# First attention of a two-block decoder: heads in pairs on half tiles of the array, mask and maximum in one VectorE instruction, softmax divided by its sum ahead of the turn, V stationary

## What is computed

```
qkv = h @ w_qkv                       # 32 query heads, 4 key/value heads, head width 64
q, k = rms_norm per head, then rope
scores = q @ k^T * 64**-0.5           # window of 128: block t=0 sees 128 keys, block t=1 sees 256
m = max(max(scores), sink)            # one learned sink a head
p = exp(scores - m)
probs = p / (sum(p) + exp(sink - m))
out = (probs @ v) @ w_o
x = x + out
```

## Time and profile before

| | us |
|---|---|
| time, median of 3 runs | 2516.59 (2515.07 to 2518.73) |
| time of the profiled execution | 2517.14 |
| its span | 2515.6 |
| TensorE busy (matmul) | 2457.2 (98%) |
| VectorE busy | 1805.7 (72%) |
| ScalarE busy | 1174.5 (47%) |
| mean granted TensorE clock | 0.992 of full speed |

### The profile page before, as it was taken

One profiled execution on the slowest core, in us unless ns is written; L12 is line 12 of the kernel. 1 busy time (PEld: TensorE's weight loads), 2 busy tenths in 40 slices (PEclk: granted clock), 3 DMA queues, 4 the chain that ended last, 5 costly groups with the idle time before them and its releaser, 6 DMA issues.

```text
span 2515.6 us, 30924 instructions
## 1 busy us (share of the span) xinstructions
PE 2457.2 (98%) x11300; PEld 2022.6 (80%) x11300; DVE 1805.7 (72%) x2444; ACT 1174.5 (47%) x1574; POOL 41.5 (2%) x62
## 2 busy tenths in 40 slices
PE   7999999999999999999999999999999789999998
PEld 6888888888888888788888888888888678888886
DVE  6655677787777787577777777778776676666655
ACT  5555544434444444454444443444444454455553
POOL 1100000000000000000000000000000000000000
PEclk9999999999999999999999999999999899999999
DMA  6433688888888887467777687767777447776653
GB/s 222 126 103 116 202 288 282 292 285 299 284 293 285 295 286 263 144 206 236 238 231 234 226 264 246 242 228 241 230 234 238 152 146 249 250 236 214 224 188 125
DMA packets 160245, 575.00 MB, mean 229 GB/s; under 512 B 17984, under 2 KB 20288, under 8 KB 160096
## 3 DMA queue, kind: packets, MB, share of 16 engines
q1 hardware_dynamic: 159280, 570.80, 68.7%
q0 software_dynamic: 816, 2.23, 0.3%
HBM read 570.86 MB, written 2.10 MB: 228 GB/s over the span
## 4 chain that ended last, share of the span: by engine, by line
PE 91%; DVE 5%; ACT 2%; issue 1%; DMA 0%; POOL 0%; SPq 0%; DVEq 0%; ACTq 0%
PE PS L926 28%; PE PS L928 28%; PE PS L927 28%; PE PS L545 2%; DVE WL L1861 1%; ACT WH L1280 1%; ACT AR L1072 0%; PE PS L621 0%; PE PS L645 0%; ACT SQ L960 0%; DVE AR L1384 0%; DVE YA L1542 0%; PE PS L885 0%; PE PS L886 0%; PE PS L832 0%
## 5 line engine op out<-in xcount | busy, mean ns | idle before, releaser
L1861 DVE TENSOR_TENSOR WL<-W,WH 128x1024 fp32r<-128x1024 f32 x816 | 991.6, 1223 | 525.9 <-ACT WH L1280 518.0
L1280 ACT ACTIVATE WH<-W 128x1024 fp32r<-128x1024 f32 x816 | 857.3, 1059 | 862.7 <-PE PS L928 855.5
L926 PE MATMUL PS<-WH,XTH 128*128 128x512 f32 x2144 | 861.6, 402 | 6.1 <-ACT WH L1280 3.2
L928 PE MATMUL PS<-WH,XTL 128*128 128x512 f32 x2144 | 838.7, 391 | 0.0
L927 PE MATMUL PS<-WL,XTH 128*128 128x512 f32 x2144 | 837.4, 391 | 0.0
L926 PEld LDWEIGHTS PS<-WH,XTH 128*128 128x128 f32 x2144 | 404.0, 188 | 91.2 <-issue 7.9
L928 PEld LDWEIGHTS PS<-WH,XTL 128*128 128x128 f32 x2144 | 403.6, 188 | 86.7
L927 PEld LDWEIGHTS PS<-WL,XTH 128*128 128x128 f32 x2144 | 404.6, 189 | 83.0 <-issue 3.8
L926 PE MATMUL PS<-WH,YTH 128*128 128x512 f32 x1120 | 442.9, 395 | 7.2 <-DVE YTL L1397 3.2
L928 PE MATMUL PS<-WH,YTL 128*128 128x512 f32 x1120 | 437.0, 390 | 0.0
L927 PE MATMUL PS<-WL,YTH 128*128 128x512 f32 x1120 | 436.5, 390 | 0.0
(11 more groups left out here) (267 smaller groups left out, 1242.3 us busy)
## 6 DMA issues: line engine op xcount, KB each, us to landing
W<-in_ada SPq DMA_DIRECT2D x192, 512.0 KB, 4.5
W<-in_avoz SPq DMA_DIRECT2D x192, 512.0 KB, 4.4
W<-in_wg SPq DMA_DIRECT2D x88, 512.0 KB, 4.8
W<-in_wu SPq DMA_DIRECT2D x88, 512.0 KB, 4.7
W<-in_wd SPq DMA_DIRECT2D x88, 512.0 KB, 5.0
W<-in_kada SPq DMA_DIRECT2D x64, 512.0 KB, 4.6
W<-in_aqk SPq DMA_DIRECT2D x64, 512.0 KB, 4.6
W<-in_aout SPq DMA_DIRECT2D x64, 512.0 KB, 4.4
```

Source lines behind the costliest of these rows:

```text
L926: e.matmul(p, x, WH[:, g % NH, j], start=first, stop=False)
L928: i = e.matmul(p, y, WH[:, g % NH, j], start=False, stop=last)
L1280: e.activation(WH[:, n % NH], W[:, i % NW], ACT.Copy).then_inc(s_hi, 1)
L1861: e.tensor_tensor(l, src, h.bitcast(F32), ALU.subtract).then_inc(s_lo, 1)
```

## The change

It touches the first attention alone.

- 24 units become 12 pairs of banks (`PAIRS`): for each group one of 8 heads for t=0, two of 4 heads for t=1. Even heads lie in rows 0 to 63 and odd ones in rows 64 to 127; the keys are kept once in both halves (K2). A score matmul uses 64 rows, even and odd heads alternate, and write two different banks.
- The mask matmul and the two memsets of KE and KO are gone. VectorE adds the mask, scales and takes the maximum together with the sink in one `tensor_tensor_reduce` a head, which writes the scaled scores to SBUF; each gives two instructions, the second reads the accumulator. ScalarE's exp then works in place in SBUF.
- A new step `scale` three ticks after the score: VectorE adds the sink's exp to the sum, inverts it, and multiplies all 1024 columns of the pair.
- `turn` transposes 8 tiles into two banks, five ticks after the score. `pv` has V stationary (64 columns) and the turned probabilities moving (512 or 256 columns), with the result already turned, in the two column halves of the array: the division, the turn of the result and `out_T` are gone.
- `attn_q` handles both row blocks one tick apart on VectorE; scores come at least 4 ticks apart; the pauses are 2 ticks and not 4.

```diff
@@ attention_order
-    while pn < 24:
+    while pn < 12:
         if pn < tn and k >= turned[pn] + 3:
             pv(pn)
             pn += 1
-        if tn < sn and tn < pn + 3 and k >= scored[tn] + 4:
+        if tn < fn and tn < pn + 2 and k >= scored[tn] + 5:
             turn(tn)
...
-        if (sn < 24 and sn < tn + 3 and k >= last + (2 if sn % 3 else 1)
-                and (sn // 6, UNITS[sn % 6][0]) in qready):
+        if fn < sn and k >= scored[fn] + 3:
+            scale(fn)
+            fn += 1
+        if sn < 12 and sn < tn + 2 and k >= last + 4 and (sn // 3, PAIRS[sn % 3][0]) in qready:
             score(sn)
@@ TensorE
-                    msk = mrow[:, 128 - 128 * t:256].unsqueeze(1).to_broadcast([128, len(hs), k])
-                    e.matmul(b[:, :].rearrange("p (a k) -> p a k", k=k), idb[:], msk, start=True, stop=False)
-                    for x, h in enumerate(hs):
-                        K = KE if h % 2 == 0 else KO
-                        i = e.matmul(b[:, k * x:k * x + k], QT[:, t, h // 2], K[:, g, 0:k], start=False,
-                                     stop=(x == len(hs) - 1))
+                    for x in range(n):
+                        for a, (b, full) in enumerate(banks):
+                            h = slice(64 * a, 64 * a + 64)
+                            i = e.matmul(b[:, k * x:k * x + k], QT[h, t, j0 + x], K2[h, g, 0:k], start=True, stop=True)
...
-                            i = e.matmul(b[:, 64 * h:64 * h + 64], PT1[N % 3][:, q:q + 128],
-                                         V1[:, k, 64 * g:64 * g + 64], start=(k == 0), stop=(k == t))
...
+                    for k in range(1 + t):
+                        for a in range(2):
+                            i = e.matmul(b[64 * a:64 * a + 64, 128 * j0:128 * j0 + m], V1[:, k, 64 * g:64 * g + 64],
+                                         PT[P % 2][a][:, m * k:m * k + m], start=(k == 0), stop=(k == t))
@@ ScalarE
-                        i = e.activation(PBL[N % 3][:, k * x:k * x + k], b[:, k * x:k * x + k], ACT.Exp,
-                                         scale=sm(u, 3)[:, h:h + 1], bias=sm(u, 6)[:, h:h + 1],
-                                         accum_out=sm(u, 7)[:, h:h + 1])
...
+                            i = e.activation(p, p, ACT.Exp, bias=sm(u, 6)[:, h:h + 1], accum_out=sm(u, 7)[:, h:h + 1])
@@ VectorE
-                e.memset(KE[64:128], 0.0)
-                e.memset(KO[0:64], 0.0).then_inc(s_kz, 1)
...
-                    step(e.tensor_reduce(mx, b[:, :].rearrange("p (a k) -> p a k", k=k), AX.X, ALU.max))
...
+                            i = e.tensor_tensor_reduce(PB[P % 2][:, 512 * a + k * x:512 * a + k * x + k],
+                                                       b[:, k * x:k * x + k], mrow[:, 128 - 128 * t:256],
+                                                       sm(u, 3)[:, h:h + 1], rows[:, RS + 8 * g + 2 * (j0 + x) + a:
+                                                                                  RS + 8 * g + 2 * (j0 + x) + a + 1],
+                                                       ALU.add, ALU.max, sm(u, 5)[:, h:h + 1])
...
+                def scale(P):
...
+                    w.wait_ge(s_p, P + 1)
+                    w.wait_ge(s_sk2, P + 1)
+                    step(e.tensor_tensor(pair(u, 10, j0, n), pair(u, 9, j0, n), pair(u, 7, j0, n), ALU.add))
                     settle()
...
+                    step(e.reciprocal(pair(u, 11, j0, n), pair(u, 10, j0, n)))
                     settle()
...
+                    p = PB[P % 2].rearrange("p (a j k) -> p a j k", a=2, k=k)
+                    e.tensor_tensor(p, p, pair(u, 11, j0, n).unsqueeze(3).to_broadcast([128, 2, n, k]),
+                                    ALU.mult).then_inc(s_pn, 1)
...
-                    e.tensor_tensor(AO[t].rearrange("p (h d) -> p h d", d=64),
-                                    b[:, :].rearrange("p (h d) -> p h d", d=64),
-                                    sm(u, 11).unsqueeze(2).to_broadcast([128, 8, 64]), ALU.mult).then_inc(s_ao, 1)
```

More of the change, by code:

```diff
@@ L657, in attn_all @@
[L657 to L666, removed]
+                    for x in range(n):
+                        for a, (b, full) in enumerate(banks):
+                            h = slice(64 * a, 64 * a + 64)
+                            i = e.matmul(b[:, k * x:k * x + k], QT[h, t, j0 + x], K2[h, g, 0:k], start=True, stop=True)
+                            if x == n - 1:
+                                i.then_inc(full, 1)
@@ L668, in ffn @@
+                yield from attention_order(score_, scale, turn, pv, qready)
             def ffn(f, slot, ver, ends, free):
@@ L1077, in turn @@
[L1077 to L1102, removed]
+                    w.wait_ge(s_ng, P + 1)
+                    for a in range(2):
+                        for x in range(n):
+                            h = 4 * a + j0 + x
+                            p = PB[P % 2][:, 512 * a + k * x:512 * a + k * x + k]
+                            i = e.activation(p, p, ACT.Exp, bias=sm(u, 6)[:, h:h + 1], accum_out=sm(u, 7)[:, h:h + 1])
@@ new lines, in score_, with scale, turn @@
+                    i.then_inc(s_p, 1)
+                    w.wait_ge(s_sk1, P + 1)
+                    e.activation(pair(u, 9, j0, n), pair(u, 8, j0, n), ACT.Exp).then_inc(s_sk2, 1)
+                def scale(P):
+                    pass
+                def turn(P):
+                    if P >= 2:
+                        w.wait_ge(s_pv, P - 1)
+                    for a in range(2):
+                        b = full(("p", P, a))
+                        e.activation(PT[P % 2][a], b[:, :], ACT.Copy).then_inc(s_pt, 1)
@@ L1533, in attn_q @@
+                yield from ticks(3)
+                for t in range(2):
+                    u = 4 * t + g
+                    w.wait_ge(s_hr, 2 + 2 * g + t + 1)
+                    e.tensor_scalar(sm(u, 3).rearrange("p (a j) -> p a j", a=2),
+                                    sm(u, 2).rearrange("p (j a) -> p a j", a=2), r8[:, t:t + 1], None,
+                                    ALU.mult).then_inc(s_qs, 1)
+                    yield
                     qready[g, t] = True
+                    yield
@@ L1572, in pv @@
-                    tasks.start(out_T(g, t))
-                yield from attention_order(score_, turn, pv, qready)
-            def out_T(g, t):
-                yield from ticks(3)
-                b = Tb[TB["ao", g, t][0]]
-                h, l = (Y[:, 4 * g:4 * g + 4, 128 * t:128 * t + 128] for Y in (YTH, YTL))
-                n_y[0] += 1
-                w.wait_ge(s_yh, n_y[0])
-                e.tensor_tensor(l, b[:, :].rearrange("p (a k) -> p a k", a=4), h.bitcast(F32),
-                                ALU.subtract).then_inc(s_yt, 1)
+                    b = Tb[TB["o", g, t][0]]
@@ L1585, in ffn @@
+                    h, l = (Y[:, 4 * g:4 * g + 4, 128 * t:128 * t + 128] for Y in (YTH, YTL))
+                    n_y[0] += 1
+                    w.wait_ge(s_yh, n_y[0])
+                    e.tensor_tensor(l, b[:, :].rearrange("p (a k) -> p a k", a=4), h.bitcast(F32),
+                                    ALU.subtract).then_inc(s_yt, 1)
+                yield from attention_order(score_, scale, turn, pv, qready)
             def ffn(f, slot, ver, ends, free):
```

192 lines of the change are left out of this document (93 added, 99 removed).

## The result

The changed kernel takes 2519.8 us (median of 20 runs, 2518.5 to 2521.55), the kernel before 2516.48 us (20 runs, 2515.07 to 2518.73): ratio 1.0014, 95% interval 1.0007 to 1.002. The change made the kernel 3.3 us slower, which lies within the 0.2% that the prediction called no change; the forecast was 2524.3 with a range of 2508 to 2537. The trace shows 11132 matmul records on TensorE where it showed 11300, 168 fewer, and the kernel ends later.

The account below looks back on a forecast made before the run. After the change, the VectorE/ScalarE chain was taken to bound the first attention. Key/value stage and groups, -3.1 + 1.7 + 4.2 + 4.7 - 3.2 = +4.3 us, plus 3.4 for the clock: +7.7 on 2516.59, 2524.3 us; range 2508 to 2537.

Parts of the forecast that it names:

- within 0.2%: Whole kernel: a time of 2511.6 to 2521.6 us, counted as no change; chance 0.24.
- The chain of VectorE and ScalarE decides: First attention: pairs strung on one chain, WL waiting for WH behind the exps; 43.4 us a group against 38.7.
- Sizes of the links: One full group, first maximum to the next group's: links of 11.6, 11.3, 12.4 and a rest of 8.2 us.
- The groups: Four first-attention stretches: 44.2, 42.3, 43.4, 42.4 us, against 42.5, 38.1, 38.7, 45.6 before.
- The clock: Groups 1 and 2: slower TensorE clock behind each group's last wait, 1.7 us each, +3.4 us.
- The key/value stage: Ahead of the first attention: without the memsets, 1.4 us of stall and 1.7 of slow clock go, -3.1 us.
- TensorE's own work: Each group: ticks, attention and transposes take 31.8 us with the array halves fully overlapping, 37.0 without.
- A PSUM bank not yet free: First attention: waits ending in an occupied PSUM bank would show the forecast wrong; put at nothing.
- No change, the rival: First attention: chain there but cheap, mask and maximum saving 7.7 us or the clock never falling (3.4); 2517, chance 0.22.

Follow-up runs that it names:

- with the memsets back: The changed kernel with two memsets of 64 x 1024 put back on VectorE in the key/value stage: 2521.64 us.
- with the halves apart: The changed kernel with score and V-product matmuls of the array's two halves no longer alternating, even heads' first, then odd heads': 2519.37 us.
- the kernel that it bounds: The changed kernel with ScalarE's exps two ticks later and VectorE's scaling two ticks after the score, not three: 2485.13 us.
- the kernel with the exps later: The changed kernel with ScalarE's exps two ticks behind VectorE's mask and maximum: 2490.84 us.

## Why the prediction was right, and which of its terms were off

The mechanism and the range held. That the range held says little by itself, since it is 29 us wide and takes in no change; of the forecast's +7.7 us, 3.3 came, so the time fell into the class "within 0.2%" (to which I had given 0.24) and not into the likelier one above it. The difference is a matter of sizes, and two of the errors partly cancel: 5.7 us too much in the four groups, and, in the profiled execution, 1.2 us too much gained ahead of them, where the full clock happened to come late:

- **The chain of VectorE and ScalarE decides.** Right, and shown: undoing what stands between the exps and the multiplication gives 17 to 35 us without a matmul less. The place, the wait of WL for WH behind the exps (3.96 us), the waits before turns (predicted some 3 us before the first and 4 before the third; measured 3.4 in group 0 and 2.0 in the others, and 3.8 in groups 1 and 2 but 1.0 in groups 0 and 3) and before the products with V are where the prediction put them.
- **Sizes of the links.** Predicted 11.6, 11.3, 12.4 and a rest of 8.2, 43.4 us; in the third group 11.1, 10.7, then 20.4 for the last two together: 42.2. The exps were too dear: I took them from rows of exps on PSUM with a scale for each row of the tile (0.44 and 0.55 each), but the new ones, in SBUF and without the scale, stand 0.385 and 0.495 apart, 0.44 us less in the first link and 0.22 in each other. Mask and maximum were right: 0.333 and 0.467 from start to start, where I had chosen 0.32 and 0.45 between bounds. The two copies add 0.95 from start to start and not 1.16.
- **The groups.** Predicted 44.2, 42.3, 43.4, 42.4, and 3.4 for the clock: 175.7. Measured 43.0, 43.7, 42.2, 41.1: 170.0. These are the terms that are off, by 5.7 us: 1.2 to 1.3 us in each of groups 0, 2 and 3 and 1.0 in group 1 (without the 2.4 us of the next point), mostly the exps, and 1.0 for the clock.
- **The clock.** Predicted +3.4 in groups 1 and 2. The granted clock shows 6.8 us lost in groups 1, 2 and 3, but the chain passes by most of it while TensorE waits anyway. It comes through where it falls behind a group's last wait. From the first maximum of the third pair to that of the next group it is 22.8 us in group 1 and 20.4 in group 2, 2.4 us once; the granted clock (third number from the end) is 0.85 in the one stretch and 1.00 in the other:

```profile
141.62:164.44 22.82, 18.32 (x95) 14.12 (x96) 14.87 (x33) 10.97 (x22) 3.27 (x2) 0.85 0.33 93
186.26:206.64 20.38, 15.85 (x95) 12.00 (x96) 14.77 (x33) 10.77 (x22) 3.27 (x2) 1.00 0.32 97
```

By this trace the term was 1.0 us too large. But the traces with the memsets back and with the halves apart have the same links, and there these two stretches take 21.75 and 22.03, and 22.02 and 22.01 us, all at 0.92: 3.0 and 3.3 us in all over twice 20.38, near the 3.4 predicted. So the 1.0 us lies within what changes from one execution to the next.
- **The key/value stage.** Predicted -3.1, of it 1.4 the wait and 1.7 the clock. The two profiled executions gave just that, the runs only 1.8 and 2.65: the wait is 1.44 to 1.5 each time, the fall of the clock behind it isn't. The term was 0.5 to 1.3 us too large.
- **TensorE's own work.** Predicted 31.8 us a group with full overlap; measured 33.0 in the kernel that it bounds. The overlap is real but not perfect: scores take 1.07 to 1.09 and products with V 1.01, where I had 0.87.
- **A PSUM bank not yet free, put at nothing.** Wrong: turns waited 3.0 us for YTL, some 1 us in each of groups 1 to 3. It is inside the second link, where YTL stood already, so it added no link, but it was a real wait. In the kernel with the exps later it is gone.
- **No change, the rival.** Its mechanism, mask and maximum at the lower price, was not what brought the time to 2519.8; the exps, the smaller prices beside them and, in this trace, 1.0 us of the clock were. That the number fell among those of this rival is not its merit.

## What to carry to other kernels

When a side engine's product becomes a step on the way to the next matmul, list what stands between its parts in the program order of each engine: here a weight conversion between two halves of a softmax lengthened the first link of a group by 2.0 us (11.1 against 9.1), and moving ScalarE's exps two ticks was worth 29 us, nine times what the whole change lost. A change that takes 5 us a group from the bounding engine can come out slower if it turns a side engine's slack into a chain; price the chain from link to link, and ask of each foreign instruction in it whether it could stand a tick earlier. A saved wait should be booked at its own length; the slower clock behind it comes in some executions and not in others.

## What the runs showed of the hardware that was not expected

- Half tiles of the array can overlap without alternating: 2 + 2 score matmuls of 256 columns take 1.07 us in either order, but 4 + 4 of 128 columns take 1.64 us against 1.09 alternating. Whether the number of matmuls in a row or their size makes the difference isn't shown.
- An f32 matmul on 64 rows alone costs as much as one on all rows, or more: read as in the earlier trace rows, from the first one's start to that of the second fp32r matmul behind them less 0.23, four of 256 columns in the same half take 84.74 - 82.48 - 0.23 = 2.03 us, 0.51 each, where two on 128 rows took 0.87, 0.44 each.
- A wait of TensorE doesn't fix the clock behind it. In the changed kernel, eight transposes took 1.97 us behind a wait of 3.83 us, and 1.09 behind one of 3.84:

```profile
153.59 1.97 PE L638 MATMUL PS<-ident,YA 128*128 128x128 f32 x8 [3.83 <-DVE YA L1565]
...
198.23 1.09 PE L638 MATMUL PS<-ident,AR 128*128 128x128 f32 x8 [3.84 <-DVE AR L1565]
```

- The exps that sum as they go have become shorter: the 128-column one shows 0.39 us where it was 0.46 before. Two things changed with them, the input (SBUF and not PSUM) and the scale for each row (gone), and no run parts them. SBUF alone is not the likely one: among ScalarE's plain conversions of 512 columns to fp32r in the same trace, the one from SBUF takes 0.63 us (line 1270), the one from PSUM 0.60 (line 1087).
- The `tensor_tensor_reduce` of 128 columns with its maximum adds 0.333 us, that of 256 columns 0.467: by these two, 0.2 us fixed and 1.05 ns a column.
